# Splitting the seams between phases into two halves of the tokens, in an fp32 transformer kernel on one core

## Chip, core and metric

The kernel runs on one core of one Trainium2 chip. The metric is the device time in microseconds, the median of a few executions. The core has TensorE (PE in the profile, its weight loads PEld), VectorE (DVE), ScalarE (ACT), GpSimd (POOL) and SyncE (SP), which here issues only the weight loads from memory.

## What is computed

512 tokens of 1024 features go through two blocks in series, all in float32. The first has an even mixer, an odd mixer and two feed-forward parts with a causal convolution. The second has, twice over, a feed-forward part (FFN), a sparse-attention mixer and another FFN. Only the second block has a normalisation behind each part as well as before it, and that is what the change is about.  One part of the second block is

```python
def rms_norm_2(x, g):
    xf = x.astype(jnp.float32)
    y = xf * lax.rsqrt(jnp.mean(xf * xf, axis=-1, keepdims=True) + EPS)
    return (y * g.astype(jnp.float32)).astype(x.dtype)

def swiglu(x, w_gate, w_up, w_down):
    return (jax.nn.silu(x @ w_gate) * (x @ w_up)) @ w_down

# one part, six times (FFN, mixer, FFN, twice)
x = x + rms_norm_2(part(rms_norm_2(x, g_pre)), g_post)
```

(for an FFN the second summand is halved). The mean runs over the 1024 features of each token, so nothing of the next part can be multiplied before the last feature of this part's result is there: the place between two parts is called a seam below.

## The kernel before

Features lie on partitions (8 tiles of 128, a K tile), tokens on the free axis (512). `x`, `h_hi`, `h_lo` and `y` are [128, 8, 512]. Every product is made three times for accuracy: an operand is split into a rounded high part and the rest, and `w_lo*h_hi`, `w_hi*h_lo`, `w_hi*h_hi` are added in PSUM. The weights come as chunks of 8 K tiles by 256 output features, 1 MB each, in a ring of four slots. SP loads a chunk when the product four chunks before is done (`chunk_done`), ACT makes `w_hi` (`split_next`, L632), POOL makes `w_lo` (L2403, four instructions a chunk). A chunk is 48 products of 512 columns (`chunk_products`, L425): 8 K tiles, two output tiles of 128 features, three each. A group is the 256 output features that share an accumulator (`main`, two PSUM banks); a `Count` object keeps the semaphore values of each engine.

The order on each engine is the order in which the code is written; every engine runs its own list and they meet at semaphores. The last part of each list around a seam:

- The result of a part is four groups (m = 0 to 3). An FFN's group has three chunks (8, 8 and 6 K tiles, `DOWN_K`), a mixer's has one. `result_scalar` squares each group's banks (L712, L715, L719, L722), `result_vector` copies them with the gain to `y` (L854, `gained`) and adds the squares up in `acc`.
- The last chunk of the last group is `chunk_halves` (L551, products L562): all K tiles of the first output tile, then all of the second. Two K tiles before the end, `first_sums` (L574) sums over the features: `token_sums` (L485) are four matmuls with one column, tokens in the stationary operand. Behind the last product come `last_sums` (L580: the second bank's squares, four more such matmuls) and `spread` (L497).
- `norm_std` on ACT makes the root (L640), `norm_diag` (L744) on DVE the reciprocal (`col`, tokens on partitions, four columns) and then four diagonal matrices `diag = ident * col` (L749). `spread` multiplies them by ones (L501), which lays one factor per token over all partitions, in the bank `m[1]`. `keep_busy` (L568, L571) puts 5 and 9 matmuls without use before and behind it.
- For each K tile DVE scales `y` (L902), adds it to `x` (L904) and makes `h_lo` (L898), while ACT makes `h_hi` (L731) and, between them, the squares of the new `x` for the next norm (L734, L736, L740). DVE adds these up (L778) and joins the two banks (`join_banks`, L770).
- `first_pair` (L510) is the next part's first two chunks side by side, K tile by K tile (L521, L522, L526): 12 products of 512 columns a tile as `h_hi` and `h_lo` come. Before the eighth tile stands `sum_squares`, which waits for the joined squares. The third chunk's K tile 1 carries the `spread` of that next norm.
- Behind the sixth part (`norm` is None) there is no next part: DVE scales and adds four pairs of tiles (L887, L891) and `last_scalar` (L2488) stores each pair.

Every other norm of the kernel (the norms before parts, the head norms of the odd mixer, two half norms in the attention mixer) uses diagonals too.

## Time and profile before

| | |
|---|---|
| median of 3 runs | 3286.05 us (3285.17 to 3287.16) |
| the profiled execution | 3287.62 us, of which the span of the core is 3285.8 us |
| PE busy | 3212.9 us, 98% of the span |
| DVE, ACT, POOL busy | 37%, 36%, 44% |
| PE products of 512 columns on line 425 | 72% of the chain of work that ended last |
| granted TensorE clock, mean | 0.991 |

PE is the engine that sets the time, so a seam is read by what PE starts when: the distance between the starts of two neighbouring products is the slot that each takes, and whatever stands between two products beyond a slot is the seam's cost. A bar's own length (0.39 us) is longer than its slot, because matmuls are pipelined. A timeline line gives start, length, engine, source line, operation, what is written and read, and in brackets the idle time before it with its releaser.

### The profile page before, as it was taken

How to read it: one execution, taken by the hardware profiler on the slowest of the kernel's cores; microseconds unless marked ns; L12 is line 12 of the kernel's file. 1: busy time of each engine (PE TensorE's matmuls, PEld its weight loads, DVE VectorE, ACT ScalarE, POOL GpSimd, SP SyncE). 2: the span in 40 equal slices, each digit the busy share in tenths (PEclk: the TensorE clock that was granted, in tenths of full speed). 3: DMA queues.
4: the chain of work that ended last, by engine and by line, in shares of the span. 5: the costliest groups of instructions: out<-in, count | busy, mean ns of one | idle time of the engine just before them, and what ended most of it. 6: DMA issues, size and time to landing. Idle time of an engine off the chain costs nothing.

```text
span 3285.8 us, 39684 instructions
## 1 busy us (share of the span) xinstructions
PE 3212.9 (98%) x15940; PEld 2643.4 (80%) x15940; DVE 1205.1 (37%) x1807; ACT 1181.5 (36%) x1404; POOL 1456.3 (44%) x1112
## 2 busy tenths in 40 slices
PE   8999999999999999999899999999999989999998
PEld 6878888888888888888776888888888877788887
DVE  6534331343433112211847522114221374752212
ACT  4544432433443233222427433224222242743322
POOL 4335444432555444444550354454444372054443
PEclk9999999999999999999999999999999999999999
DMA  4213222211222222223320132222222241022222
GB/s 147 78 52 107 97 100 105 100 59 65 95 97 100 105 97 95 102 91 114 130 81 22 52 116 89 102 103 90 98 94 103 85 154 69 5 99 90 102 97 96
DMA packets 46235, 302.57 MB, mean 92 GB/s; under 512 B 5392, under 2 KB 7440, under 8 KB 10784
## 3 DMA queue, kind: packets, MB, share of 16 engines
q1 hardware_dynamic: 41040, 292.79, 24.9%
q10 hardware_dynamic: 5072, 7.96, 0.8%
q8 instruction: 99, 1.62, 0.2%
q14 instruction: 24, 0.20, 0.0%
HBM read 296.54 MB, written 2.10 MB: 91 GB/s over the span
## 4 chain that ended last, share of the span: by engine, by line
PE 89%; DVE 7%; ACT 2%; DMA 1%; issue 1%; ACTq 0%; DVEq 0%; SPq 0%
PE main L425 72%; PE main L442 3%; PE main L562 2%; PE main L1923 1%; PE misc L485 1%; PE main L521 1%; PE main L522 1%; PE main L526 1%; PE misc L521 1%; PE misc L522 1%; PE misc L526 1%; DVE b_p L2298 1%; ACT b_p L2079 1%; DVE b_flat L2164 1%; DMA stage<-in_w 0%
## 5 line engine op out<-in xcount | busy, mean ns | idle before, releaser
L2403 POOL TENSOR_TENSOR w_lo<-stage,w_hi 128x512 fp32r<-128x512 f32 x1104 | 1451.0, 1347 | 1793.5 <-ACT w_hi L632 1793.0
L425 PE MATMUL main<-h_hi,w_lo 128*128 128x512 f32 x2456 | 966.2, 393 | 8.6 <-DVE val L2111 6.3
L425 PE MATMUL main<-h_hi,w_hi 128*128 128x512 f32 x2456 | 960.5, 391 | 0.0
L425 PE MATMUL main<-h_lo,w_hi 128*128 128x512 f32 x2456 | 960.5, 391 | 0.0
L632 ACT ACTIVATE w_hi<-stage 128x2048 fp32r<-128x2048 f32 x276 | 524.7, 1909 | 408.6 <-DMA stage<-in_w 407.7
L425 PEld LDWEIGHTS main<-h_hi,w_lo 128*128 128x128 f32 x2456 | 464.2, 189 | 108.8 <-DVE val L2111 6.8
L425 PEld LDWEIGHTS main<-h_hi,w_hi 128*128 128x128 f32 x2456 | 463.8, 189 | 97.1
L425 PEld LDWEIGHTS main<-h_lo,w_hi 128*128 128x128 f32 x2456 | 464.3, 189 | 96.0 <-issue 0.5
L425 PE MATMUL main<-hid_hi,w_lo 128*128 128x512 f32 x1168 | 454.5, 389 | 0.0
L425 PE MATMUL main<-hid_hi,w_hi 128*128 128x512 f32 x1168 | 454.4, 389 | 0.0
L425 PE MATMUL main<-hid_lo,w_hi 128*128 128x512 f32 x1168 | 454.4, 389 | 0.0
L425 PEld LDWEIGHTS main<-hid_hi,w_lo 128*128 128x128 f32 x1168 | 219.3, 188 | 45.9 <-issue 0.2
L425 PEld LDWEIGHTS main<-hid_lo,w_hi 128*128 128x128 f32 x1168 | 219.3, 188 | 45.4
L425 PEld LDWEIGHTS main<-hid_hi,w_hi 128*128 128x128 f32 x1168 | 219.3, 188 | 45.3
L821 DVE TENSOR_TENSOR val<-main,rstd 128x1024 f32<-128x1024 f32 x60 | 73.5, 1224 | 461.4 <-PE main L425 461.4
L685 ACT ACTIVATE hid_hi<-val 128x1024 f32 (+1 forms) x66 | 69.9, 1059 | 372.2 <-DVE val L827 372.2
L801 DVE TENSOR_TENSOR gate<-main,rstd 128x1024 f32<-128x1024 f32 x66 | 80.8, 1225 | 318.5 <-PE main L425 301.7
L854 DVE TENSOR_SCALAR y<-main,par 128x512 f32<-128x512 f32 x48 | 36.0, 750 | 378.2 <-PE main L425 330.2
L831 DVE TENSOR_TENSOR hid_lo<-val,hid_hi 128x1024 f32 (+1 forms) x66 | 89.4, 1355 | 91.2 <-ACT hid_hi L685 91.2
L680 ACT ACTIVATE sq<-gate 128x1024 f32<-128x1024 f32 x44 | 46.7, 1061 | 185.5 <-DVE gate L819 185.0
L846 DVE TENSOR_TENSOR x<-main,x 128x1024 f32<-128x1024 f32 x16 | 19.6, 1225 | 245.8 <-PE main L425 245.8
L814 DVE SCALAR_TENSOR_TENSOR sq<-gate,par,sq 128x512 f32<-128x512 f32 x88 | 72.6, 846 | 45.2 <-ACT sq L673 39.1
(342 smaller groups left out, 3242.2 us busy)
## 6 DMA issues: line engine op xcount, KB each, us to landing
stage<-in_w SPq DMA_DIRECT2D x276, 1024.0 KB, 4.8
x<-in_xT SPq DMA_DIRECT2D x4, 512.0 KB, 8.1
out_x<-x ACTq DMA_DIRECT2D x4, 512.0 KB, 2.7
stage<-in_w SPq DMA_DIRECT2D x4, 256.0 KB, 8.2
b_r<-sq ACTq DMA_DIRECT2D x4, 256.0 KB, 6.9
b_r<-sq ACTq DMA_DIRECT2D x4, 255.5 KB, 8.4
ev_ws<-in_ev_ws ACTq DMA_DIRECT2D x1, 512.0 KB, 7.0
b_pos<-in_pos ACTq DMA_DIRECT2D x2, 256.0 KB, 2.7
```

Of the source, the lines that this page charges most:

```text
L425: last = pe.matmul(acc[:, m, :], w[a], r[b], start=start and k == 0 and j == 0, stop=stop and k == nk - 1 and j == 2)
L442: last = pe.matmul(out, x[:, k, r], w[:, s, k, :], start=k == 0 and t % 2 == 0 and j == 0, stop=k == KT - 1 and t % 2 == 1 and j == 2)
L521: pe.matmul(accs[j][:, m, :], w[1], c.h_hi[:, k, :], start=k == 0, stop=False)
L522: pe.matmul(accs[j][:, m, :], w[0], c.h_hi[:, k, :], start=False, stop=False)
L526: last = pe.matmul(accs[j][:, m, :], c.w_hi[:, slots[j], k, m * P:(m + 1) * P], c.h_lo[:, k, :], start=False, stop=k == KT - 1)
L632: act.activation(c.w_hi[:, s, :, :].rearrange("p k n -> p (k n)"), c.stage[:, s, :], ACT.Copy)\
L685: e.activation(two(c.hid_hi, i), c.val[:, :, :], ACT.Copy).then_inc(c.hid_hi_done, 1)
L801: e.tensor_tensor(c.gate[:, :, 2:], c.ps[n.slot()][:, :, :], rstd, ALU.mult)\
L814: e.scalar_tensor_tensor(c.sq[:, j, :], c.gate[:, j, k:k + T], c.par[:, bass.ds(col + 2 * i + j, 1)], c.sq[:, j, :], ALU.mult, ALU.add).th ...
L821: e.tensor_tensor(c.val[:, :, :], (c.mp[1] if extra else c.ps[n.slot()])[:, :, :], rstd, ALU.mult)\
L831: e.tensor_tensor(two(c.hid_lo, i), c.val[:, :, :], two(c.hid_hi, i).bitcast(F32), ALU.subtract).then_inc(c.hid_lo_done, 1)
L2403: last = e.tensor_tensor(c.w_lo[:, s, k:k + 2, :].rearrange("p k n -> p (k n)"), c.stage[:, s, k * CW:(k + 2) * CW], c.w_hi[:, s, k:k + 2, ...
```

## The change

Three things are changed together.

1. **The last result group is done in token halves.** The 512 tokens are cut into two `HALF`s of 256. All products of the last group's chunks are made at 256 columns (`half_products`), each half accumulating in its own PSUM bank: first half 0 of all chunks, then half 1. Half 0's squares, sums (`half_sums`, six matmuls now in place of four, since DVE no longer adds the last squares to `acc`), root, reciprocal and `half_spread` are hung between the products of half 1 (`half_hooks`, at the fifth and twelfth K step).
2. **The next pair takes four K tiles in halves.** `first_pair` walks K tiles 0 to 3 for half 0, then the same for half 1 (again 256 columns), then tiles 4 to 7 at 512. The sums and the spread of half 1 stand before its second and third step. DVE and ACT follow the same walk: scale, add, `h_hi`, `h_lo` of four half tiles, then those of half 1, then full tiles. `keep_busy` is gone from the seam. At the very end of the kernel the elementwise work and the stores are cut in halves too.
3. **Factors are spread without diagonals,** in every norm of the kernel: the stationary operand is one column of the factor repeated 128 times, the moving one is the identity (`spread_columns`). The four diagonal instructions on DVE (on ACT in the odd mixer) are gone.

```diff
+def spread_columns(pe, c, bank, cols):
+    for i in range(TT):
+        last = pe.matmul(bank[:, i * P:(i + 1) * P], cols[:, i:i + 1].to_broadcast([P, P]), c.ident[:, :],
+                         start=True, stop=True)
+    return last
 def spread(pe, n, c):
-    for i in range(TT):
-        pe.wait_ge(c.diag_ready, n(c.diag_ready))
-        last = pe.matmul(c.m[1][:, i * P:(i + 1) * P], c.ones[:, :], c.diag[:, i, :], start=True, stop=True)
-    last.then_inc(c.spread_ready, 1)
+    pe.wait_ge(c.rstd_ready, n(c.rstd_ready))
+    spread_columns(pe, c, c.m[1], c.col[:, 0:4]).then_inc(c.spread_ready, 1)
...
-    for k in range(KT):
-        if k == KT - 1:
+    walk = [(k, slice(0, T)) for k in range(KT)]
+    if n.halves:
+        walk = [(k, cols) for cols in HALF for k in range(EARLY)] + walk[EARLY:]
+    for p, (k, cols) in enumerate(walk):
+        if n.halves and p == 1:
+            half_sums(pe, n, c, 1)
+        if n.halves and p == 2:
...
+        if final:
             sum_squares(pe, n, c)
...
-                pe.matmul(accs[j][:, m, :], w[1], c.h_hi[:, k, :], start=k == 0, stop=False)
-                pe.matmul(accs[j][:, m, :], w[0], c.h_hi[:, k, :], start=False, stop=False)
+                pe.matmul(accs[j][:, m, cols], w[1], c.h_hi[:, k, cols], start=p == 0, stop=False)
+                pe.matmul(accs[j][:, m, cols], w[0], c.h_hi[:, k, cols], start=False, stop=False)
...
+HALF = (slice(0, CW), slice(CW, T))
+EARLY = 4
+def half_products(pe, c, acc, hi, lo, s, nk, k0, half, start, stop, at={}):
     for m in range(2):
         for k in range(nk):
-            if m == 1 and k == nk - 2:
...
+            if m * nk + k in at:
+                at[m * nk + k]()
+            out = acc[:, half, m * CW:(m + 1) * CW]
             w = (c.w_hi[:, s, k, m * P:(m + 1) * P], c.w_lo[:, s, k, m * P:(m + 1) * P])
-            r = (hi[:, k0 + k, :], lo[:, k0 + k, :])
+            r = (hi[:, k0 + k, HALF[half]], lo[:, k0 + k, HALF[half]])
...
-                last = pe.matmul(acc[:, m, :], w[a], r[b], start=start and k == 0 and j == 0,
-                                 stop=k == nk - 1 and j == 2)
-        last.then_inc((c.bank0_done, c.chunk_done)[m], 1)
...
+    return last
+def half_columns(c, half):
+    return c.m[0][:, 0:2] if half == 0 else c.m[1][:, T - 2:T]
+def half_sums(pe, n, c, half):
+    pe.wait_ge((c.p_sqa, c.p_sqb)[half], n((c.p_sqa, c.p_sqb)[half], 4))
+    src = [c.acc[:, 0, HALF[half]], c.sq[:, half, HALF[0]], c.sq[:, half, HALF[1]]]
+    for q, x in enumerate(src):
+        for u in range(2):
+            last = pe.matmul(half_columns(c, half)[:, u:u + 1], x[:, u * P:(u + 1) * P], c.ones[:, 0:1],
+                             start=q == 0 and u == 0, stop=q == 2 and u == 1)
+    last.then_inc(c.ssq_ready, 1)
+def half_bank(c, half):
+    return c.m[0][:, HALF[1]] if half == 0 else c.m[1][:, HALF[0]]
+def half_spread(pe, n, c, half):
+    pe.wait_ge(c.rstd_ready, n(c.rstd_ready))
+    for u in range(2):
+        last = pe.matmul(half_bank(c, half)[:, u * P:(u + 1) * P],
+                         c.col[:, 2 * half + u:2 * half + u + 1].to_broadcast([P, P]), c.ident[:, :],
+                         start=True, stop=True)
+    last.then_inc(c.spread_ready, 1)
...
-def last_sums(pe, n, c):
-    pe.wait_ge(c.p_sqb, n(c.p_sqb, 4))
-    token_sums(pe, c.m[0], c.ones, c.sq[:, 1, :], False, True).then_inc(c.ssq_ready, 1)
-    keep_busy(pe, c, 5)
-    spread(pe, n, c)
-    keep_busy(pe, c, 9)
+def half_hooks(pe, n, c, sums, spread):
+    def first():
+        pe.wait_ge(c.p_total, n(c.p_total))
+        half_sums(pe, n, c, 0)
+    return {sums: first, spread: lambda: half_spread(pe, n, c, 0)}
...
-            if post is not None and g == 3 and j == 2:
-                chunk_halves(pe, n, c, acc, c.hid_hi, c.hid_lo, nk, 8 * j, False, lambda: first_sums(pe, n, c))
-            else:
-                chunk_products(pe, n, c, acc, c.hid_hi, c.hid_lo, nk, 8 * j, j == 0, j == 2)
-    if post is not None:
-        last_sums(pe, n, c)
+            chunk_products(pe, n, c, acc, c.hid_hi, c.hid_lo, nk, 8 * j, j == 0, j == 2)
+    n.halves = post is not None
+    if post is None:
+        return
+    slots = [(n.chunk + j) % RING for j in range(3)]
+    def part(j, half, at={}):
+        return half_products(pe, c, acc, c.hid_hi, c.hid_lo, slots[j], DOWN_K[j], 8 * j, half, j == 0, j == 2, at)
+    pe.wait_ge(c.w_lo_done, n(c.w_lo_done))
+    part(0, 0)
+    part(0, 1).then_inc(c.chunk_done, 1)
+    pe.wait_ge(c.w_lo_done, n(c.w_lo_done))
+    part(1, 0)
+    pe.wait_ge(c.w_lo_done, n(c.w_lo_done))
+    part(2, 0).then_inc(c.bank0_done, 1)
+    part(1, 1, half_hooks(pe, n, c, 4, 11)).then_inc(c.chunk_done, 1)
...
         else:
+            act.wait_ge(c.p_add, n(c.p_add))
+            act.activation(c.col[:, 4:5], c.eps, ACT.Sqrt)
             act.wait_ge(c.bank0_done, n(c.bank0_done))
-            act.wait_ge(c.p_add, n(c.p_add))
             act.activation(c.sq[:, 0, :], acc[:, 0, :], ACT.Square).then_inc(c.p_sqa, 1)
-            act.activation(c.col[:, 4:5], c.eps, ACT.Sqrt)
-            act.wait_ge(c.chunk_done, n.chunk - AHEAD)
-            act.activation(c.sq[:, 1, :], acc[:, 1, :], ACT.Square).then_inc(c.p_sqb, 1)
+    def std(half):
+        u = slice(2 * half, 2 * half + 2)
+        act.wait_ge(c.ssq_ready, n(c.ssq_ready))
+        act.activation(c.col[:, u], half_columns(c, half), ACT.Sqrt, bias=c.eps, scale=1.0 / D).then_inc(c.std_ready, 1)
...
+    def second_squares():
+        act.wait_ge(c.chunk_done, n.chunk - AHEAD)
+        act.activation(c.sq[:, 1, :], acc[:, 1, :], ACT.Square).then_inc(c.p_sqb, 1)
     n.skip(c.group_taken, 4)
-    norm_std(act, n, c)
-    n.skip(c.spread_ready)
+    n.skip(c.spread_ready, 2)
+    std(0)
     if norm is None:
+        second_squares()
+        std(1)
         return
-    for k in range(KT):
+    def high(k, cols):
         act.wait_ge(c.x_ready, n(c.x_ready))
         col = PC["norm"] + norm * 8 + k
...
+    for k in range(EARLY):
+        high(k, HALF[0])
+    second_squares()
+    std(1)
+    for k in range(KT):
+        high(k, HALF[1] if k < EARLY else slice(0, T))
+        next_squares(act, n, c, k)
     n.skip(c.acc_ready, 2)
...
+            dve.tensor_tensor(c.acc[:, 0, :], c.acc[:, 0, :], c.acc[:, 1, :], ALU.add).then_inc(c.p_total, 1)
             n.skip(c.chunk_done)
...
+    def gained_half(half):
+        col = PC["post"] + post * 8 + 6
+        dve.wait_ge((c.p_sqa, c.p_sqb)[half], n((c.p_sqa, c.p_sqb)[half]))
+        for b in range(2):
+            last = dve.tensor_scalar(c.y[:, 6 + b, HALF[half]], acc[:, half, b * CW:(b + 1) * CW],
+                                     c.par[:, col + b:col + b + 1], None, ALU.mult)
+        last.then_inc(c.post_y if half == 0 else c.group_taken, 1)
+    def half_rstd(half):
+        u = slice(2 * half, 2 * half + 2)
+        dve.wait_ge(c.std_ready, n(c.std_ready))
+        dve.reciprocal(c.col[:, u], c.col[:, u]).then_inc(c.rstd_ready, 1)
+    gained_half(0)
+    dve.wait_ge(c.post_y, n(c.post_y))
+    half_rstd(0)
...
+        for half in range(2):
+            if half == 1:
+                gained_half(1)
+                dve.wait_ge(c.group_taken, n(c.group_taken, 0))
+                half_rstd(1)
+            dve.wait_ge(c.spread_ready, n(c.spread_ready))
+            for m in range(4):
+                y, x = (two(t, m)[:, :, HALF[half]] for t in (c.y, c.x))
+                dve.tensor_tensor(y, y, over_tiles(half_bank(c, half)), ALU.mult).then_inc(c.post_y, 1)
...
+    def gain(k, cols, factor):
+        dve.tensor_tensor(c.y[:, k, cols], c.y[:, k, cols], factor, ALU.mult).then_inc(c.post_y, 1)
+        dve.wait_ge(c.post_y, n(c.post_y))
+        dve.tensor_tensor(c.x[:, k, cols], c.x[:, k, cols], c.y[:, k, cols], ALU.add).then_inc(c.x_ready, 1)
+        n.skip(c.x_ready)
+    dve.wait_ge(c.spread_ready, n(c.spread_ready))
+    for k in range(EARLY):
+        gain(k, HALF[0], half_bank(c, 0))
+        if k >= 1:
+            low(k - 1, HALF[0])
+    low(EARLY - 1, HALF[0])
+    gained_half(1)
+    half_rstd(1)
+    dve.wait_ge(c.group_taken, n(c.group_taken, 0))
+    dve.wait_ge(c.spread_ready, n(c.spread_ready))
+    both = c.mp[0][:, :, :].rearrange("p b t -> p (b t)")[:, CW:CW + T]
     for k in range(KT):
-        dve.tensor_tensor(c.y[:, k, :], c.y[:, k, :], c.m[1][:, :], ALU.mult).then_inc(c.post_y, 1)
-        dve.wait_ge(c.post_y, n(c.post_y))
-        dve.tensor_tensor(c.x[:, k, :], c.x[:, k, :], c.y[:, k, :], ALU.add).then_inc(c.x_ready, 1)
-        n.skip(c.x_ready)
+        if k < EARLY:
+            gain(k, HALF[1], half_bank(c, 1))
+        else:
+            gain(k, slice(0, T), both)
         if k == 7:
             dve.wait_ge(c.x_ready, n(c.x_ready, 0))
         if k >= 1:
-            low(k - 1)
+            low(k - 1, HALF[1] if k <= EARLY else slice(0, T))
         if k in (5, 7):
             gather_squares(dve, n, c, k // 2 - 1)
-    low(7)
...
     chunk_products(pe, n, c, group_slot(pe, n, c), c.hid_hi, c.hid_lo, KT)
-    chunk_halves(pe, n, c, group_slot(pe, n, c), c.hid_hi, c.hid_lo, KT, 0, True, lambda: first_sums(pe, n, c))
-    last_sums(pe, n, c)
+    acc = group_slot(pe, n, c)
+    pe.wait_ge(c.w_lo_done, n(c.w_lo_done))
+    s = n.chunk % RING
+    half_products(pe, c, acc, c.hid_hi, c.hid_lo, s, KT, 0, 0, True, True).then_inc(c.bank0_done, 1)
+    half_products(pe, c, acc, c.hid_hi, c.hid_lo, s, KT, 0, 1, True, True, half_hooks(pe, n, c, 4, 11))\
+        .then_inc(c.chunk_done, 1)
+    n.chunk += 1
...
-    act.wait_ge(c.stored, 64)
+    for half in range(2):
+        for m in range(4):
+            act.wait_ge(c.last_ready, 4 * half + m + 1)
+            act.dma_start(out[:, 2 * m:2 * m + 2, HALF[half]], c.x[:, 2 * m:2 * m + 2, HALF[half]])\
+                .then_inc(c.stored, 16)
+    act.wait_ge(c.stored, 128)
```

The other diagonals (odd mixer on ACT, attention mixer on DVE) are removed in the same way; the weight ring and the loops inside the parts are as they were.

On PE, around the first seam (FFN to mixer), the end of the last group before, where L485 are sums, L571 fillers, L501 the spread and L521 the pair:

```order
L485 MATMUL misc<-ones,acc 128x1 x4
L562 MATMUL main<-hid_hi,w_lo 128x512
L562 MATMUL main<-hid_lo,w_hi 128x512
L562 MATMUL main<-hid_hi,w_hi 128x512
L562 MATMUL main<-hid_hi,w_lo 128x512
L562 MATMUL main<-hid_lo,w_hi 128x512
L562 MATMUL main<-hid_hi,w_hi 128x512
L485 MATMUL misc<-ones,sq 128x1 x4
L571 MATMUL misc<-ones,ident 128x128 x5
L501 MATMUL misc<-diag,ones 128x128 x4
L571 MATMUL misc<-ones,ident 128x128 x9
L521 MATMUL main<-h_hi,w_lo 128x512
```

and the same place after, at the mixer-to-FFN seam where the rows are shortest: L561 the last product of half 1, L535, L536 and L540 the pair's first and second half tile, L577 the six sums of half 1, L591 its spread comes one half tile later:

```order
L561 MATMUL main<-hid_hi,w_hi 128x256
L535 MATMUL main<-h_hi,w_lo 128x256
L536 MATMUL main<-h_hi,w_hi 128x256
L535 MATMUL main<-h_hi,w_lo 128x256
L536 MATMUL main<-h_hi,w_hi 128x256
L535 MATMUL misc<-h_hi,w_lo 128x256
L536 MATMUL misc<-h_hi,w_hi 128x256
L535 MATMUL misc<-h_hi,w_lo 128x256
L536 MATMUL misc<-h_hi,w_hi 128x256
L540 MATMUL main<-h_lo,w_hi 128x256 x2
L540 MATMUL misc<-h_lo,w_hi 128x256 x2
L577 MATMUL misc<-ones,acc 128x1 x2
```

Nothing stands between the last result product and the pair's first any more; the sums moved behind the pair's first half tile.

On DVE the same seam before, from the gain of the last bank (L854) over the reciprocal (L746) and the diagonals (L749) to the second K tile:

```order
L854 TENSOR_SCALAR y<-main,par 128x512 x2
L746 RECIPROCAL col<-col 128x4
L749 TENSOR_SCALAR diag<-ident,col 128x128 x4
L902 TENSOR_TENSOR y<-y,misc 128x512
L904 TENSOR_TENSOR x<-x,y 128x512
L902 TENSOR_TENSOR y<-y,misc 128x512
L904 TENSOR_TENSOR x<-x,y 128x512
L898 SCALAR_TENSOR_TENSOR h_lo<-x,par,h_hi 128x512
```

and after, from half 0's last `h_lo` (L965) through the gain of half 1 (L936) and its reciprocal (L943) to its first tiles (L969, L971):

```order
L971 TENSOR_TENSOR x<-x,y 128x256
L965 SCALAR_TENSOR_TENSOR h_lo<-x,par,h_hi 128x256 x2
L936 TENSOR_SCALAR y<-main,par 128x256 x2
L943 RECIPROCAL col<-col 128x2
L969 TENSOR_TENSOR y<-y,misc 128x256
L971 TENSOR_TENSOR x<-x,y 128x256
```

Half 0's chain stands ahead of all of half 1's on DVE. ACT has the same order: here the first four `h_hi` halves (L781) stand ahead of the squares of half 1 (L769), between the two roots (L765):

```order
L760 ACTIVATE sq<-main 128x512
L765 ACTIVATE col<-misc,stat 128x2
L781 ACTIVATE h_hi<-x,par 128x256 x4
L769 ACTIVATE sq<-main 128x512
L765 ACTIVATE col<-misc,stat 128x2
```

Before, the squares of the last bank had nothing but the other bank's squares and a constant's root ahead of them.

## Rows read from the trace of the kernel before

**Rows 1.** The page: span, and busy time of PE.

```profile
span 3285.8 us, 39684 instructions
PE 3212.9 (98%) x15940; PEld 2643.4 (80%) x15940; DVE 1205.1 (37%) x1807; ACT 1181.5 (36%) x1404; POOL 1456.3 (44%) x1112
```

**Rows 2.** Timeline of the first seam, FFN to mixer, PE, ACT and DVE.

```profile
1553.69 0.39 PE L562 MATMUL main<-hid_hi,w_hi 128*128 128x512 f32 x1
...
1554.72 0.49 PE L562 MATMUL main<-hid_hi,w_lo 128*128 128x512 f32 x1
...
1555.97 0.40 PE L562 MATMUL main<-hid_hi,w_hi 128*128 128x512 f32 x1
1556.41 0.60 ACT L722 ACTIVATE sq<-main 128x512 f32<-128x512 f32 x1 [2.90 <-PE main L562]
...
1560.27 0.69 DVE L902 TENSOR_TENSOR y<-y,misc 128x512 f32<-128x512 f32 x1 [0.66 <-PE misc L501]
...
1562.58 0.47 PE L521 MATMUL main<-h_hi,w_lo 128*128 128x512 f32 x1 [0.34 <-ACT h_hi L731]
```

**Rows 3.** The same timeline at the end of the pair.

```profile
1575.37 0.69 DVE L904 TENSOR_TENSOR x<-x,y 128x512 f32<-128x512 f32 x1
...
1579.66 5.47 POOL L2403 TENSOR_TENSOR w_lo<-stage,w_hi 128x512 fp32r<-128x512 f32 x4 [31.41 <-ACT w_hi L632]
...
1579.82 1.68 DVE L770 TENSOR_TENSOR acc<-acc 128x512 f32<-128x512 f32 x1
...
1585.40 0.40 PE L425 MATMUL main<-h_hi,w_lo 128*128 128x512 f32 x1
```

**Rows 4.** The chain that ended last: start, length, products without a gap.

```profile
71.65 11.50 PE main L442 x96
...
1219.50 327.78 PE main L425 x1446
```

**Rows 5.** Groups by line and shape: operations of 256 columns.

```profile
L2298 DVE CUSTOM_DVE_ANT_0 b_p<-main,b_amask 128x256 f32<-128x256 f32 x32 | 11.6, 421 | 0.0
L1565 DVE SCALAR_TENSOR_TENSOR od_s<-od_s,od_decays,misc 128x256 f32<-128x256 f32 x24 | 11.5, 481 | 5.6 <-PE misc L1332 3.8 <-DVE acc L1598 0.8 <-DVE val L1598 0.2
L2079 ACT ACTIVATE b_p<-b_p,b_nmax 128x256 f32<-128x256 f32 x32 | 15.8, 503 | 0.0
```

**Rows 6.** Timeline of the first mixer-to-FFN seam, PE.

```profile
1859.41 0.40 PE L562 MATMUL main<-hid_hi,w_hi 128*128 128x512 f32 x1
...
1866.01 0.47 PE L521 MATMUL main<-h_hi,w_lo 128*128 128x512 f32 x1 [0.34 <-ACT h_hi L731]
```

**Rows 7.** Timeline of the kernel's end: last product, first and last elementwise work.

```profile
3269.11 0.40 PE L562 MATMUL main<-hid_hi,w_hi 128*128 128x512 f32 x1
...
3273.39 2.35 DVE L887 TENSOR_TENSOR y<-y,misc 128x1024 f32<-128x1024 f32 x2 [0.66 <-PE misc L501]
...
3280.20 2.36 DVE L891 TENSOR_TENSOR x<-x,y 128x1024 f32<-128x1024 f32 x2
```

**Rows 8.** Timelines where diagonals are made: odd mixer, attention mixer, an FFN's third chunk.

```profile
687.81 1.16 PE L1379 MATMUL misc<-diag,ones 128*128 128x128 f32 x8 [2.19 <-ACT diag L1443]
...
1762.50 1.16 PE L1860 MATMUL misc<-diag,ones 128*128 128x128 f32 x8 [0.71 <-DVE diag L2316]
...
1890.19 0.83 PE L501 MATMUL misc<-diag,ones 128*128 128x128 f32 x6
...
1891.44 0.47 PE L425 MATMUL main<-h_hi,w_lo 128*128 128x512 f32 x1
```

**Rows 9.** Busy time in stretches of the odd mixer: PE, PEld, DVE, ACT, POOL, granted clock.

```profile
684.00:688.00 4.00, 1.81 (x9) 1.19 (x8) 1.74 (x3) 3.48 (x7) 3.27 (x3) 1.00 0.00 0
...
720.00:724.00 4.00, 4.00 (x13) 3.09 (x12) 0.18 (x1) 2.93 (x7) 3.86 (x4) 0.57 0.01 4
```

**Rows 10.** The chain again, in the odd mixer, ahead of the second stretch.

```profile
711.84 1.50 PE main L442 x12
...
717.05 1.95 PE misc L485 x16
```

153 lines of the change are left out of this document (49 added, 104 removed).

## The prediction, as it was made before the changed kernel ran

> **What bounds the kernel now.** I read the page first: PE is busy 98% of the span [rows 1], so an edit pays only where it shortens the distance between two PE products. Then the chain that ended last, for the price of a product: 1446 products of 512 columns took 327.78 us without a gap, 0.2267 us each, and 96 products of 256 columns took 11.50 us, 0.1198 us each [rows 4]. So a full product cut in two costs 2 x 0.1198 - 0.2267 = 0.0129 us more. Then the timeline of a seam. From the start of the last result product to the pair's first pass 1562.58 - 1555.97 = 6.61 us, of which 0.23 is a slot: 6.38 us of standing or filling [rows 2]. The mixer's seam has 1866.01 - 1859.41 = 6.60 [rows 6]; all five inner seams are alike. The first sums, in the stream, take the way from 1553.69 to 1555.97 for six slots, 2.28 - 1.36 = 0.92 us [rows 2]. A seam costs 7.30 us, five of them 36.5 us, and the end of the kernel has its own tail. That is all the change can reach, apart from the diagonals.
>
> **What an FFN seam costs after.** Three FFN seams (22 K tiles in the last group).
> - Width: 22 x 6 = 132 result products and 4 x 12 = 48 of the pair are cut in two: 180 x 0.0129 = 2.32 us.
> - Sums and spreads now all stand in the stream. The four sums cost 0.92, so about 0.20 each and 0.1 for the start; six cost 1.31, twice: 2.62. Two spread matmuls at the same 0.20: 0.50, twice: 1.00. The new stationary operand (one column repeated) has no row; bounds are the same price as the diagonal and twice the 0.20, which adds 0.8 us to a seam. I take the same, since the rows with a full 128x128 stationary show no dependence on the moving width.
> - The wait at the pair's first product. Let the last product of half 0 end its slot at 0. Squares (0.2 later, 0.60 long) are done at 0.9, before the sums' place at 12 x 0.12 = 1.44; sums end at 2.75, root and reciprocal at 3.5, and the spread stands at 1.44 + 1.31 + 21 x 0.12 = 5.27, so the factor is readable at about 5.9. Scale and add at 256 columns take 0.42 each (the PSUM reader of that width 421 ns, a three-operand one 481, ACT 503 [rows 5], against 0.69 at 512 [rows 2]): `x` at 6.8, `h_hi` at 7.4. The pair starts at (48 + 36) x 0.12 + 1.31 + 0.50 = 11.9. Nothing waits, with 4.4 us to spare. This is the cover that hides the whole first half; without it the 6.38 us come back.
> - The wait behind it. DVE needs, before, from its first scaling at 1560.27 to the end of the last `x` at 1576.06 15.8 us, and 5.44 more until the squares are joined at 1579.82 + 1.68 = 1581.50 [rows 2, 3]. PE reached its sums just then, without a wait. After, twelve of DVE's instructions (four tiles, three each) are half as wide and 0.265 shorter: 15.8 - 3.2 + 5.44 = 18.05 us from the spread of half 1. But PE has less to do in that time: 24 half products (2.88), 48 more (5.75) and 36 full ones (8.16), 16.8, less 0.18 until the factor can be read, 16.6. So PE stands 1.4 us before the eighth tile: half of the pair's DVE work used to run ahead of the pair, now only a part of it does. The third chunk's `w_lo`, ready 0.27 before its use [rows 3], moves with the same `x` and comes out level with PE again: no second wait.
> Sum: 2.32 + 2.62 + 1.00 + 1.4 = 7.34 against 7.30: nothing. The bound from below on the last wait is 0, if DVE's half instructions are shorter than the nearest rows, from above 2.4.
>
> **A mixer seam** (two of them) has 8 K tiles: 48 + 48 products cut, 1.24 us; sums and spreads 3.62; the wait at the eighth tile 1.4. The pair starts already at 48 x 0.12 + 1.81 = 7.6, just when the first half `h_hi` is there (7.4). But then come, on ACT and in this order, four half `h_hi` and only then half 1's squares. DVE needs 5.9 + 4.2 us for four tiles with their `h_lo`, so the fourth `h_hi` is done at 10.6 and the squares at 11.2. PE wants them at 7.6 + 1.44 = 9.1: it stands 2.1 us with the rest of the pair queued behind it. Sum 8.36 against 7.30: +1.06 each. Inner seams together: 3 x 0.04 + 2 x 1.06 = **+2.2 us**.
>
> **The end.** Width 132 x 0.0129 = 1.70; the sums and spread of half 0 in the stream 1.81 in place of 0.92: +0.9. From the last product at 3269.11 to the first scaling at 3273.39 pass 4.28 us [rows 7]; the sums get 0.4 longer, the spread 0.4 shorter, the first diagonal goes: -0.3. The elementwise work behind it, 3273.39 to 3282.56, 9.2 us for eight instructions of 1024 columns [rows 7], becomes eight of 512 in dependent pairs, 8 x 0.69 = 5.5: -3.7. The last store is half as large: 0 to -0.7, say -0.4. Together **-1.8 us**.
>
> **Diagonals.** Where PE waited for them they go: odd mixer 2.19 us of waiting [rows 8], of which the four ACT instructions are 1.3; attention mixer 0.71 us of wait and as long a DVE share behind it, 0.8 each, two times. In the third chunk of an FFN POOL runs beside and the four diagonals are late: the spread holds the stream 1.25 us, from 1890.19 to 1891.44, instead of 0.81 [rows 8]; that is 0.44 in three such places and about 0.5 in the odd mixer's. The others are made long before their use and are worth nothing. -1.3 - 1.6 - 1.8 = **-4.7 us**, between -2 and -6.
>
> **Sum:** 2.2 - 1.8 - 4.7 = -4.3 us. The profiled execution took 3287.62 us with 3285.8 of span; a like one would take 3283.3. The median of the runs is 1.57 below it, so the forecast for the median is 3286.05 - 4.3 = 3281.8 us.
>
> One rule is to be weighed. The rows give a slot of 0.2267 us at 512 columns and 0.1198 at 256 [rows 4], that is 13 ns above the columns at 2.4 GHz whatever the width. The Trainium skill, page "TensorE: Matmul & The Clock Gate", section "Back-to-back issue gap", gives 2.5 ns for that; by it a cut product costs 2.5 ns more and not 12.9, and the 864 cut products 2 us and not 11: 3272.8 us. The trace disagrees with the page, and the sum goes by the trace.
>
> **Rivals.**
> - *The cover holds and no wait takes its place.* If DVE's half instructions and ACT's order leave no wait at the eighth tile (5 x 1.4) and at the mixer's sums (2 x 2.1), 11.2 us more go: 3270.6. For it: I built both waits on prices taken from other lines. Against: they rest on rows of just this width [rows 5], and 1.4 us is a quarter of what DVE would have to gain. A part of it would already be measurable: 2.3 us below my forecast. In the same direction goes a smaller price of width, as above. Chance 0.29.
> - *The clock falls at the seams.* The fillers that kept PE at work are gone, and the standing at the eighth tile and at the mixer's sums comes right beside one-column sums. The granted clock fell to 0.57 over 4 us after PE had stood from 713.34 to 717.05, 3.7 us [rows 9, 10], which costs 1.7 us of products; around the wait of 2.2 us it was 1.00 [rows 8, 9]. With 1.7 us behind each of the seven standings: 3281.8 + 12 = 3294: slower. It decides from standings of between 2.2 and 3.7 us; mine are 1.4 and 2.1. Chance 0.08. The Trainium skill says the same direction, in the same page's section "Why this matters for your kernels": avoid idle gaps of TensorE between bursts of matmuls, or it goes back to the half clock.
> - *A half product waits for its stationary operand.* The weight load is 0.19 us long in the trace, longer than the 0.12 slot. If it did not overlap here, all 1728 half products would cost 0.07 more, +121 us: 3403. The 96 products of 256 columns at 0.1198 [rows 4] load a stationary as large and speak plainly against. With a slower column load of the spreads in it: chance 0.04.
> - *The pair is not released early*, since half 0's factor comes too late: the mixer seam has 0.2 us to spare there. 1 us late would add 2 us: 3284, inside my range.
>
> **How the numbers follow.** Forecast 3281.8, chance 0.59 with what the unknown prices leave around it (3279.5 to 3290). A difference under 0.2%, 6.6 us, is about what a measurement of this kernel can't tell from no change: faster is below 3279.5, slower above 3292.6. Faster 0.29 (the first rival, whole or half), same 0.59, slower 0.12 (clock, stationary operand). The range 3272 to 3290 leaves out the whole of the first rival below and the two slower ones above.
>
> **What would show it.** In the profile after: products of L561 and the pair's 256-column ones 0.12 us apart; the pair's first product one slot behind the last of L561; a wait of about 1.4 us at the sums before the eighth tile, five times, on DVE's L826; a wait of about 2.1 us at L577 in the two mixer seams, on ACT's L769; the spreads with the column at 0.10 us a record; the granted clock 1.00 across each seam; the distance from the last product to the span's end shorter by some 4 us. The prediction is wrong if one of the two waits is missing, if the clock falls, or if other work behind the seam moves, such as a weight chunk that comes late in the third chunk.

## The result, and the profile after

The changed kernel is slower: 3289.71 us (median of 20 runs, 3285.72 to 3295.71) beside 3283.82 us for the kernel before (20 runs), ratio 1.0017, 95% interval 1.0011 to 1.0023: +5.9 us where -4.3 was forecast. That is within the 0.2% called "same", but on the other side of zero. One execution of one kernel below (`cover_tile8`) took 9404 us at a granted clock of 0.332; the ratios leave it out.

The page of the changed kernel, as [rows 1] was of the one before:

```profile
span 3293.0 us, 41186 instructions
...
PE 3220.2 (98%) x16684; PEld 2684.1 (82%) x16684; DVE 1179.1 (36%) x1807; ACT 1183.9 (36%) x1414; POOL 1457.7 (44%) x1112
```

The span of the profiled execution is 7.2 us longer than that of before. Most of what the forecast built is there. PE's timeline of the first seam, where [rows 2] showed 6.61 us between the last product and the pair's first (start, length, engine, line, operation):

```profile
1558.55 0.28 PE L561 MATMUL main<-hid_hi,w_hi 128*128 128x256 f32 x1
1558.67 0.28 PE L535 MATMUL main<-h_hi,w_lo 128*128 128x256 f32 x1
...
1560.11 0.50 PE L577 MATMUL misc<-ones,acc 128*128 128x1 f32 x4
1560.47 1.03 PE L577 MATMUL misc<-ones,sq 128*128 128x1 f32 x8
...
1562.88 0.60 PE L591 MATMUL misc<-ident,col 128*128 128x128 f32 x4
```

The pair starts one slot of 0.12 us behind the last result product. The two waits that the forecast put in its place are there too, at their sizes. PE's waits (who waits for whom: total, times, longest):

```profile
PE misc L485 <- DVE acc L826: 6.7, 6, 1.4
...
PE misc L577 <- ACT sq L769: 4.5, 3, 1.9
```

1.35 us before the eighth K tile (forecast 1.4), 1.9 at half 1's sums in the two mixer seams (forecast 2.1; the third is the end's 0.69). Where the new time lies is read from one event that both kernels have, the sums before the eighth tile, at the five seams; first before, then after:

```profile
1581.74 0.95 PE L485 MATMUL misc<-ones,acc 128*128 128x1 f32 x8
...
1885.18 0.95 PE L485 MATMUL misc<-ones,acc 128*128 128x1 f32 x8
...
2253.94 0.95 PE L485 MATMUL misc<-ones,acc 128*128 128x1 f32 x8
...
2622.70 0.95 PE L485 MATMUL misc<-ones,acc 128*128 128x1 f32 x8
...
2926.11 0.95 PE L485 MATMUL misc<-ones,acc 128*128 128x1 f32 x8
```

```profile
1581.66 1.05 PE L485 MATMUL misc<-ones,acc 128*128 128x1 f32 x8 [1.35 <-DVE acc L826]
...
1891.19 1.05 PE L485 MATMUL misc<-ones,acc 128*128 128x1 f32 x8 [0.91 <-DVE acc L826]
...
2259.73 0.49 PE L485 MATMUL misc<-ones,acc 128*128 128x1 f32 x3 [1.36 <-DVE acc L826]
...
2628.24 1.05 PE L485 MATMUL misc<-ones,acc 128*128 128x1 f32 x8 [1.35 <-DVE acc L826]
...
2933.54 1.05 PE L485 MATMUL misc<-ones,acc 128*128 128x1 f32 x8 [1.35 <-DVE acc L826]
```

The differences are -0.1, +6.0, +5.8, +5.5 and +7.4 us: the two FFN seams in the middle add nothing (-0.2 and -0.3, of which -0.4 each is the third chunk without its diagonals); the loss lies between the first pair's eighth tile and the first mixer seam's, and again from the second mixer on. The stretches there, with the granted clock (PE, PEld, DVE, ACT and POOL busy, then the granted clock, third from the right, and the DMA):

```profile
1580.00:1584.00 4.00, 2.65 (x16) 2.11 (x15) 1.79 (x3) 0.26 (x1) 4.00 (x4) 0.98 0.10 7
1584.00:1588.00 4.00, 4.00 (x13) 3.14 (x12) 0.00 (x0) 0.00 (x0) 1.21 (x1) 0.60 0.36 99
1864.00:1868.00 4.00, 2.11 (x16) 1.90 (x14) 3.47 (x9) 1.50 (x3) 0.00 (x0) 0.89 0.72 262
1868.00:1872.00 4.00, 4.00 (x20) 4.00 (x21) 0.17 (x1) 0.26 (x1) 0.00 (x0) 0.50 0.00 0
1872.00:1876.00 4.00, 4.00 (x28) 4.00 (x28) 2.79 (x8) 1.70 (x3) 0.00 (x0) 0.76 0.00 0
...
2932.00:2936.00 4.00, 2.65 (x15) 2.17 (x15) 1.67 (x2) 1.65 (x2) 4.00 (x4) 0.94 0.00 0
2936.00:2940.00 4.00, 4.00 (x13) 3.15 (x12) 0.00 (x0) 0.00 (x0) 4.00 (x4) 0.64 0.16 20
```

Three times the clock goes down to its lower level of 1.2 GHz right behind one of the new standings (behind the eighth tile's at 1581.66 and 2933.54, behind the 1.9 us at 1866.86), and (1 - clock) x 4 us summed over each group gives 1.7, 3.4 and 1.7 us, 6.8 in all. (Inside the first mixer, ahead of 1753 us, the distance to before grew by another 1.4 us. Before has two falls of the clock there and this trace has four, besides the one at 1584 us; that they are the 1.4 us is argued, not shown.) From the sums at 2926.11 and 2933.54 to the end of the span are 359.7 us before and 359.5 after; the later one contains the third of these falls (+1.7) and a third chunk without diagonals (-0.4), so the end itself gave -1.5. From the last result product to the span's end pass 12.5 us where it was 16.7, the 4 us less that the forecast named.

### The profile page after: what moved, and what is told of

It reads as the page before. It is cut to its first block, busy times and chain, and to the rows that moved or that the text cites. A ratio compares the mean times of both kernels' runs of the same rounds, so it can differ in the third digit from the quotient of the medians.

```text
span 3293.0 us, 41186 instructions
## 1 busy us (share of the span) xinstructions
PE 3220.2 (98%) x16684; PEld 2684.1 (82%) x16684; DVE 1179.1 (36%) x1807; ACT 1183.9 (36%) x1414; POOL 1457.7 (44%) x1112
## 4 chain that ended last, share of the span: by engine, by line
PE 88%; DVE 9%; ACT 2%; issue 1%; DMA 0%; SPq 0%; DVEq 0%; ACTq 0%
PE main L425 70%; PE main L561 4%; PE main L442 3%; PE main L1992 1%; DVE acc L834 1%; ACT b_p L2152 1%; DVE x L971 1%; DVE y L969 1%; DVE b_p L2371 1%; PE misc L485 1%; DVE h_lo L965 1%; PE main L535 1%; PE misc L500 1%; PE misc L577 1%; PE misc L1872 0%
## 5 line engine op out<-in xcount | busy, mean ns | idle before, releaser
L425 PE MATMUL main<-hid_hi,w_lo 128*128 128x512 f32 x1040 | 404.7, 389 | 0.0
L425 PE MATMUL main<-hid_hi,w_hi 128*128 128x512 f32 x1040 | 404.6, 389 | 0.0
L425 PE MATMUL main<-hid_lo,w_hi 128*128 128x512 f32 x1040 | 404.6, 389 | 0.0
L425 PEld LDWEIGHTS main<-hid_hi,w_lo 128*128 128x128 f32 x1040 | 195.2, 188 | 40.7 <-issue 0.2
L425 PEld LDWEIGHTS main<-hid_lo,w_hi 128*128 128x128 f32 x1040 | 195.2, 188 | 40.6
L425 PEld LDWEIGHTS main<-hid_hi,w_hi 128*128 128x128 f32 x1040 | 195.2, 188 | 40.5
L910 DVE TENSOR_SCALAR y<-main,par 128x512 f32<-128x512 f32 x36 | 27.0, 751 | 354.0 <-PE main L425 330.3
L561 PE MATMUL main<-hid_hi,w_lo 128*128 128x256 f32 x416 | 118.7, 285 | 0.0
L561 PE MATMUL main<-hid_hi,w_hi 128*128 128x256 f32 x416 | 117.7, 283 | 0.0
L561 PE MATMUL main<-hid_lo,w_hi 128*128 128x256 f32 x416 | 117.7, 283 | 0.0
```

Source lines behind the costliest of these rows:

```text
L425: last = pe.matmul(acc[:, m, :], w[a], r[b], start=start and k == 0 and j == 0, stop=stop and k == nk - 1 and j == 2)
L561: last = pe.matmul(out, w[a], r[b], start=start and m == 0 and k == 0 and j == 0, stop=stop and m == 1 and k == nk - 1 and j == 2)
```

## Experiments

A standing is a stretch in which PE waits with nothing to do; a fall is a stretch at the lower clock; a cover is work without use that fills a standing. Two theories at the start. **A:** PE's standings of 1 to 2 us bring the clock down, and the fillers (`keep_busy`) and the old order kept it up at the seams. **B:** the falls of the clock come and go by themselves, and a kernel of other timing meets others. "Against the changed kernel" is a difference of two ratios to before, times 3284 us; an interval of such a difference is about 4 us wide on either side of nothing, so only the larger ones say much by themselves.

**The spreads alone**, the third part of the change in the kernel before.

> The kernel before with nothing changed but the factors: no diagonals, each spread is a product of the broadcast column and the identity. The forecast took this part for -4.7 us (odd mixer -1.3, attention mixers 2 x -0.8, three third chunks and one place of the odd mixer -1.8). Theory A (the clock takes back what the odd mixer gains: PE still stands 1 us before the head's sums, the clock falls behind it and comes back at the same moment of the program as in the kernel before): the odd mixer gives nothing at its end, the attention mixers 2 x -0.8, the third chunks -0.4 each: -2.5 us, between -1.5 and -3.3, and a granted clock of under 0.65 in 716 to 724 us. Theory B (the clock plays no part in it; what went missing in the changed kernel went missing in the seams): -4.7 us, between -4 and -5.5, and the 1.7 us gained by 717 us are still there at 725 us.

```diff
+    pe.wait_ge(c.rstd_ready, n(c.rstd_ready))
+    spread_columns(pe, c, c.m[1], c.col[:, 0:4]).then_inc(c.spread_ready, 1)
...
```

Measured: 3278.58 us, ratio 0.9983 (0.9974 to 0.9992), -5.6 us. The median lies at the forecast's -4.7 and theory B's range; the interval, -8.5 to -2.6, also reaches into theory A's (-1.5 to -3.3), so the time alone does not decide. The traces speak against "given back": the same product runs 4.5 us earlier than in before both ahead of head 1's sums (684.73 and 689.27 us) and behind the fall (719.23 and 723.74), and each trace has one fall there. But they also say how such a thing arises. Clock in the odd mixer of before, beside [rows 9], and then of the spreads alone:

```profile
752.00:756.00 4.00, 3.02 (x19) 2.66 (x18) 0.20 (x1) 3.75 (x3) 0.83 (x1) 0.81 0.47 199
756.00:760.00 4.00, 4.00 (x10) 3.13 (x11) 0.18 (x1) 3.22 (x7) 4.00 (x4) 0.50 0.00 0
760.00:764.00 4.00, 4.00 (x21) 3.16 (x21) 1.22 (x1) 0.00 (x0) 0.13 (x1) 0.84 0.00 0
```

```profile
752.00:756.00 4.00, 4.00 (x17) 3.28 (x16) 0.18 (x1) 1.43 (x2) 3.63 (x3) 0.61 0.00 0
```

The same standing (head 2's, 0.98 us) is followed by (0.19 + 0.50 + 0.16) x 4 = 3.4 us of lost clock in one execution and by (0.04 + 0.39) x 4 = 1.7 in the other, whose clock is 0.96 in the 4 us ahead of this row and 1.00 in the next rows.

**Before without its fillers.**

> The kernel before without its 5 + 9 filling products at each post-norm seam; nothing else changed. They write a bank that nobody reads. Theory A (standings beside one-column sums bring the clock down, and the fillers kept it up): behind most of the five inner seams the products run at half rate for 3 us or so, 1.7 us each at least; +5 to +12 us, granted clock of about 0.6 in the 4 us behind a seam. Theory B (the clock's falls in the changed kernel come from when its standings happen, not from missing fillers): within 1 us of before, the clock 1.00 behind the seams as it is now.

```diff
...
-    keep_busy(pe, c, 5)
     spread(pe, n, c)
-    keep_busy(pe, c, 9)
```

Measured: 3298.85 us, ratio 1.0042 (1.0028 to 1.0056), +13.8 us, a little above the upper end of theory A. Where the fillers stood PE now stands, and the clock falls behind it:

```profile
PE main L521 <- ACT h_hi L729: 11.8, 5, 2.4
...
PE misc L501 <- DVE diag L747: 6.4, 9, 1.0
```

```profile
1552.00:1556.00 4.00, 1.65 (x9) 1.39 (x9) 3.27 (x6) 1.14 (x2) 0.00 (x0) 0.78 0.35 145
1556.00:1560.00 4.00, 4.00 (x11) 3.03 (x11) 3.93 (x7) 2.42 (x4) 0.00 (x0) 0.50 0.02 4
```

It fell so at all five inner seams. In the seams as they were, with PE waiting up to 2.4 us for the pair's first operand, the fillers that the change removed were worth 14 us, and no line of the forecast's sum had them. What they would be worth in the new seams, where the pair waits for nothing, this run does not show. The same pair of traces speaks for a part of B: up to 1553 us the two programs are alike instruction by instruction, yet the sums that stand at 1213.41 us in before stand at 1205.96 here:

```profile
1205.96 0.95 PE L485 MATMUL misc<-ones,acc 128*128 128x1 f32 x8
```

7.45 us between two executions of the same code, 6.7 of them in three places where the clock fell in the one (at 24 to 36, 720 to 724 and 752 to 764 us) and not at all in the other.

**The changed kernel with its standings covered.**

> The changed kernel with cover where PE stands in its inner seams: six products of 512 columns (1.36 us, into the result slot that is already free) ahead of the sums before the eighth K tile in all five seams, and in the two mixer seams sixteen repeats of the pair's first 256-column product (1.92 us) before the pair. Nothing else is changed; the waits of 1.4 and 1.9 us shrink to 0 to 0.4. Theory A: the granted clock stays at 1.00 through the seams that lost 1.7, 4.0 and 2.9 us, and 5 to 8 us of the time come back: 3282 to 3285 us for a kernel that takes 3289.7, about 1.000 of before. Theory B: the clock falls all the same, or the fillers only push the pair back: no gain, 3289 to 3292 us, 1.0015 to 1.0025 of before.

```diff
         if final:
+            if n.halves:
+                pe.wait_ge(c.group_taken, n(c.group_taken, 0))
+                for _ in range(6):
+                    pe.matmul(c.ps[n.slot()][:, 0, :], c.w_hi[:, slots[0], 0, 0:P], c.h_hi[:, 0, :],
+                              start=True, stop=True)
             sum_squares(pe, n, c)
         pe.wait_ge(c.h_hi_done, n(c.h_hi_done))
+        if p == 0:
+            for _ in range(n.fill):
+                pe.matmul(accs[0][:, 0, cols], c.w_lo[:, slots[0], k, 0:P], c.h_hi[:, k, cols], start=True, stop=True)
```

(`n.fill` is 16 in the mixer seams and 0 in the others.) Measured: 3280.24 us, ratio 0.9989 (0.9980 to 0.9998): -9.2 us against the changed kernel, from products that compute nothing. The stretch that had 0.98 and 0.60, and the mixer seam:

```profile
1576.00:1580.00 4.00, 4.00 (x21) 3.30 (x21) 0.18 (x1) 0.27 (x1) 3.13 (x3) 1.00 0.25 82
...
1856.00:1860.00 4.00, 4.00 (x34) 3.83 (x33) 1.97 (x6) 1.26 (x3) 0.00 (x0) 1.00 0.54 229
```

No seam of this trace has a clock under 1.00. Theory A holds for the seams.

**Only the eighth tile covered** (the first hunk alone), to tell the standings of 1.35 us from those of 1.9.

> The changed kernel with only the first half of the cover: six products of 512 columns (1.36 us) ahead of the sums before the eighth K tile in the five inner seams; the mixer seams' wait of 1.9 us at half 1's sums stays uncovered. In the trace of the changed kernel the clock fell behind the eighth tile's standing in the first FFN seam (1580 to 1588) and in the second mixer seam (2932 to 2940), and behind the standing of 1.9 us in the first mixer seam (1864 to 1876). Theory A1 (a standing of 1.4 us is enough when one-column sums follow it): the falls behind the eighth tile are gone, that behind the 1.9 us stays: 4 to 6 of the 9 us that the full cover gave, 3283.5 to 3286 us. Theory A2 (only the standings of 1.9 us matter): 0 to 2 us, 3287.5 to 3290 us.

Measured: 3283.72 us, ratio 1.0001 (0.9991 to 1.0010), -5.3 us against the changed kernel; the other cover is the remaining -3.9. That is theory A1's forecast (3283.5 to 3286): standings of 1.35 us are enough. In its trace both uncovered mixer seams lose clock, the first as in the changed kernel:

```profile
1852.00:1856.00 4.00, 2.13 (x16) 1.93 (x15) 3.75 (x10) 1.82 (x4) 0.00 (x0) 0.92 0.66 240
1856.00:1860.00 4.00, 4.00 (x20) 4.00 (x21) 0.25 (x2) 0.26 (x1) 0.00 (x0) 0.50 0.06 23
```

**Half 1's squares earlier in the mixer seams.**

> The changed kernel with ACT's order changed in the two mixer seams alone: half 1's squares between the second and the third half h_hi, not behind the fourth. The forecast's account of the 1.9 us wait (ACT's order sets it) says: the sums are ready when PE comes to them. DVE still makes half 1's reciprocal only after its four tiles, done some 6.3 us after the first gain; PE, 1.9 us earlier at the spread, stands there for 0.6 to 0.8 us. So 1.9 turns into 0.7: -1.2 us each, -2.4 in all, and with the shorter standing the clock may stay up behind one or both seams, up to 3 us more: 3284.5 to 3287.5 us. Against it, if DVE sets the wait and not ACT's order: the whole 1.9 us comes back at the spread, 3289 to 3290.5 us.

```diff
     for k in range(EARLY):
+        if k == EARLY - 2 and chunks == 1:
+            second_squares()
         high(k, HALF[0])
-    second_squares()
+    if chunks > 1:
+        second_squares()
```

Measured: 3284.01 us, ratio 0.9993 (0.9984 to 1.0002), -7.9 us against the changed kernel, at the good end and beyond. ACT's order did set the wait, and it is gone whole; of the 0.6 to 0.8 us that I expected at the spread only 0.2 came:

```profile
1861.52 1.03 PE L577 MATMUL misc<-ones,sq 128*128 128x1 f32 x8
...
1864.10 0.71 PE L591 MATMUL misc<-ident,col 128*128 128x128 f32 x4
```

Neither line has a wait at its end, and the spread starts 0.18 us later behind the products ahead of it than in the first FFN seam. 2 x 1.9 us are saved, and with them the fall behind. Not every fall goes with them: behind the eighth tile's standing of the second seam, 1.36 us here, the clock now falls (at 1884 us), where it had stood only 0.91 us and kept its clock in the changed kernel.

**Products between the one-column sums**, the standing left as it is.

> The changed kernel with the 1.4 us before the eighth tile's sums left standing, but with one product of 512 columns behind each of the four one-column sums (4 x 0.23 us more work in each of five seams, up to +4.5 us). It asks whether the standing or the one-column sums behind it bring the clock down. If the standing alone does: the falls stay, 1.0017 of before plus 0.0013: 3293 to 3294.5 us. If it takes the sums' 0.9 us of nearly idle engine as well: the falls behind the eighth tile go as in cover_tile8 (-5.2 us) and 4.5 are paid: 3288.5 to 3290 us, and the clock is 1.00 at 1580 to 1592 us and behind the second mixer seam's eighth tile.

```diff
+def spaced_sums(pe, n, c, slot):
...
+    for i in range(TT):
+        last = pe.matmul(c.m[0][:, i:i + 1], c.acc[:, 0, i * P:(i + 1) * P], c.ones[:, 0:1],
+                         start=i == 0, stop=i == TT - 1)
+        pe.matmul(c.ps[n.slot()][:, 0, :], c.w_hi[:, slot, 0, 0:P], c.h_hi[:, 0, :], start=True, stop=True)
...
-        if final:
+        if final and n.halves:
+            spaced_sums(pe, n, c, slots[0])
+        elif final:
             sum_squares(pe, n, c)
```

Measured: 3292.66 us, ratio 1.0024 (1.0014 to 1.0035), the median nearer to "the standing alone" (3293) than to the other (3290), the interval too wide to decide. The trace decides the place:

```profile
1577.56 0.38 PE L496 MATMUL misc<-ones,acc 128*128 128x1 f32 x2 [1.35 <-DVE acc L840]
1577.80 0.48 PE L498 MATMUL main<-h_hi,w_hi 128*128 128x512 f32 x1
...
1579.78 0.63 PE L550 MATMUL main<-h_hi,w_hi 128*128 128x512 f32 x1
1580.21 0.63 PE L549 MATMUL main<-h_hi,w_lo 128*128 128x512 f32 x1
```

With wide products among the sums the clock still fell: from 1579.8 a product takes 0.43 us and not 0.23. At this place the standing does it without the sums' nearly idle engine. At the second mixer seam the fall behind the eighth tile was absent, but PE had stood less there than in the changed kernel (1.35 us), because a fall of the clock ahead had made it late:

```profile
2931.81 0.38 PE L496 MATMUL misc<-ones,acc 128*128 128x1 f32 x2 [1.06 <-DVE acc L840]
```

So for the other seams the question stays open.

**Head 0's sums one K tile later in the odd mixer.**

> The changed kernel with head 0's sums in the odd mixer one K tile later (6 products of 0.23 us moved ahead of them) and its spread one tile later too. Nothing else is changed. PE stood 1.0 us there, with the clock at 0.60 and 0.54 in 716 to 724 us behind it. Theory A: without the standing the clock stays at 1.00 there, the 1.7 us that the absent diagonals gave are kept, and the standing itself goes: -1.7 - 1.0 = -2.7 us against the changed kernel, between -2 and -4. Theory B (the clock falls behind the sixteen one-column sums themselves, with or without a standing): -1.0 us, between 0 and -1.2, and the clock under 0.65 as before.

```diff
-    z(at={2: lambda: sums(0), 5: lambda: spread_head(0)})
+    z(at={3: lambda: sums(0), 6: lambda: spread_head(0)})
```

Measured: 3286.36 us, ratio 1.0002 (0.9993 to 1.0011), -4.9 us (by the medians -3.3; theory A had -2 to -4). The size fits within the noise, the reason given does not: I had taken the sums at 717 us for head 0's, and they are head 1's. Head 0's stood 1.0 us at 679 us, with the clock at 1.00 behind. Head 1's standing is still there in this run's trace (0.98 us at 713.80), and the clock does not fall behind it.

**The best of the parts.** Three more kernels put together what paid: first the spreads and the end in halves, with the inner seams of before.

> The kernel before with the spreads by columns and with the last seam alone, the one behind which no pair follows, in token halves: 132 products of the last group cut in two, sums, factor, scaling and stores by half. The five inner seams are as before, with their fillers. The forecast's price of the end is -1.8 us (in the trace of the changed kernel -1.95): 3278.6 - 1.9 = 3276.7 us, 0.9975 to 0.998 of before. If the halves at the end only looked cheap because the changed kernel's clock was lower or higher there: no difference from the spreads alone, 3278 to 3279 us.

Measured: 3279.41 us, ratio 0.9980 (0.9971 to 0.9989). Against the spreads alone that is -1.0 us by the ratios and +0.8 by the medians: not told apart, and above the 3276.7 that was expected. In the traces the distance from the last seam's sums (2915.13 and 2921.89 us) to the span's end is 359.4 and 357.7 us, -1.7, as priced.

> As spreads_end, and in the odd mixer head 0's sums and spread one K tile later (as in odd_later). There that gave 3.3 us against the changed kernel by the medians, 1.0 us of it the standing. If the clock's fall behind that standing is what the rest was: again -2.7 to -3.3, 3273.5 to 3274.5 us, and the granted clock of 712 to 724 us is 1.00. If the gain in odd_later was the run's luck: -1.0, 3275.7 us. Both kernels would then be slower than this one by 0.3%.

Measured: 3275.05 us, ratio 0.9974 (0.9964 to 0.9985), between the two values that were expected, 3274.5 and 3275.7: undecided. Its PE row for head 1 and the clock behind it, and then the same with head 1's sums moved too:

```profile
714.02 1.95 PE L485 MATMUL misc<-ones,sq 128*128 128x1 f32 x16 [0.98 <-ACT sq L1548]
...
716.00:720.00 4.00, 4.00 (x19) 3.29 (x18) 0.18 (x1) 2.61 (x3) 4.00 (x4) 1.00 0.02 4
```

> spreads_end_odd with head 1's sums and spread one K tile later as well. A correction to what was expected of odd_later belongs here: head 0's sums are those at 679 us of the trace of before, and the ones at 717 us, behind which the clock was at 0.57, are head 1's. Moving head 0's took away a standing of 1.0 us at 679 us; that of head 1 was still there (0.98 us at 714.0) and the clock nevertheless stayed at 1.00 behind it in that trace, as it had not in seven of the nine others. So a standing of 1 us brings the clock down in some executions and not in others. If that is so, head 1's move gives its 1.0 us and the share of executions in which the clock fell there, some 0.7 x 1.5 to 2 us: -2 to -2.5 us, 3272.5 to 3273 us, and clock 1.00 in 708 to 724 us. If the clock falls behind the sixteen one-column sums alone: -1.0 us, 3274 us, and the clock under 0.7 at 712 to 720 us.

```diff
-    z(at={2: lambda: sums(1), 5: lambda: spread_head(1)})
+    z(at={3: lambda: sums(1), 6: lambda: spread_head(1)})
```

```profile
713.25 1.84 PE L485 MATMUL misc<-ones,sq 128*128 128x1 f32 x16
...
716.00:720.00 4.00, 4.00 (x24) 3.45 (x22) 0.18 (x1) 1.63 (x3) 3.88 (x4) 1.00 0.00 0
```

Measured: 3273.13 us, ratio 0.9967 (0.9957 to 0.9976): faster than before by 10.8 us, and than the changed kernel by 16. It is the fastest of the study. Against spreads_end_odd it is -2.3 us, as expected, but too little to be told from nothing by itself. The sixteen sums without a standing leave the clock at 1.00; with the standing it was 1.00 in the trace above too, so this pair does not separate the two.

> The changed kernel with three repairs together: six filling products of 512 columns before the eighth tile's sums (cover_tile8), half 1's squares earlier in the mixer seams (squares_early; there the wait of 1.9 us went to zero), and head 0's sums and spread in the odd mixer one K tile later (odd_later). Against the full cover (0.9989 of before), in which the 1.9 us were filled and not saved: -2 x 1.9 us for the squares, -1.5 to -3.3 us for head 0: 3274 to 3276 us, 0.9967 to 0.9975 of before. If the three gains were only luck of the clock, each taking back the other's: 3279 to 3281 us. Beside spreads_end_odd (the same kernel with the inner seams of before, 0.9974) it tells what the halves of the inner seams are worth once they are covered: by the sum 3 x +0.25 for the FFN seams and 2 x -0.75 for the mixer seams, -0.75 us, so nothing that can be told from zero.

Measured: 3275.90 us, ratio 0.9976 (0.9967 to 0.9985), at the upper end of what was expected (3276 us, 0.9975). With every repair the halves in the inner seams end where the old inner seams with their fillers are (0.9974): their worth is not told from nothing, +0.02% with an interval of 0.14% to either side.

**Theory A and B together.** In the odd mixer the standing is always 0.98 us. Over the twelve other traces (all but odd_later_two), head 1's, at some 713 to 717 us, was followed by a fall of the clock in 9; head 2's, near 750 us, in 8 of 13; head 0's, near 679 us, in 1 of the 9 traces that have it. Before the eighth tile there are 20 uncovered places (four kernels, five seams). In 16 of them PE stood 1.34 to 1.37 us, and a fall followed in 8: in all four first seams, in the four mixer seams among them, and in none of the eight middle FFN seams. In the other 4, mixer seams behind a fall at half 1's sums, it stood 0.45 to 1.06 us, and no fall followed. The uncovered 1.9 us were followed by one in 6 of 8. So a standing does bring the clock down (A), but not each, and not equally long (what B had right). Why the middle seams differ so steadily from the others was not settled.

## Why the prediction was wrong

By its steps, in order. **Slots and widths** held: 0.12 us a half product, the pair one slot behind. **Seams**, read from the covered kernel against the spreads alone, between the same sums on either side (both have the spreads): the three FFN seams +0.05, +0.27 and +0.21 us where +0.04 was forecast, the two mixer seams +1.13 and +1.16 where it was +1.06. **The waits**, 1.4 and 2.1: 1.35 and 1.9, on the lines named. **The end**, -1.8: -1.5 here, -1.7 in spreads_end. **Diagonals**, -4.7: -5.6, with an interval of 3 us to either side; in the traces the wait in the odd mixer gave 1.3, as forecast, and the third chunk's spread holds the stream 0.81 us, from 1896.36 to 1897.17, where it was 1.25 (forecast -0.44). The spread by a column costs as much as the one by a diagonal, as assumed; [rows 8] has its answer here:

```profile
686.09 1.16 PE L500 MATMUL misc<-ident,stat 128*128 128x128 f32 x8 [0.90 <-DVE stat L1656]
...
1896.36 1.05 PE L500 MATMUL misc<-ident,col 128*128 128x128 f32 x8
```

2.19 us of wait have become 0.90 (forecast -1.3).

Together these give what the forecast's sum says, and they are not what failed. Take the ratios: the change as a whole is +5.6 us, the spreads are -5.6 and the end some -1.5, so the inner seams cost +12.7, give or take 4, where the sum had +2.2. With cover they cost 9.2 less, +3.5. **The clock at the seams is the rest**: the second rival was the case. It had +12 us for seven falls of 1.7; 9.2 came back with the cover. The changed kernel's one trace has three falls there, 6.8 us, and grew by another 1.4 us in the first mixer, which no run isolates.

The step that failed is this one: "The granted clock fell to 0.57 over 4 us after PE had stood from 713.34 to 717.05, 3.7 us", and with it "It decides from standings of between 2.2 and 3.7 us; mine are 1.4 and 2.1", which pressed the rival's chance to 0.08. PE did not stand for 3.7 us there. The numbers come from the chain of work that ended last [rows 10]; it leaves PE at 713.34 because the sums were waiting for DVE and ACT, and says nothing of what PE did meanwhile. PE's own timeline of before does:

```profile
715.68 0.39 PE L425 MATMUL main<-h_hi,w_hi 128*128 128x512 f32 x1
717.05 1.95 PE L485 MATMUL misc<-ones,sq 128*128 128x1 f32 x16 [0.98 <-ACT sq L1433]
```

It worked until 716.07 and stood 0.98 us. A fall behind 0.98 us stood in the trace of before; read so, both new standings lie above the least that was seen to matter, and the rival had to be weighed like the forecast itself. The one clear place of 2.2 us without a fall [rows 8, 9] showed only that not every standing does it. A second omission goes with it: the 5 + 9 fillers were priced by the time that they free and not by what they keep up, which no_fillers puts at 13.8 us for the old seams.

The Trainium skill, page "TensorE: Matmul & The Clock Gate", section "HAM oscillation — how this bites in real kernels", tells of a kernel whose every K tile starts at the lower clock because PE waits between tiles. That is the direction seen here; its waits are longer than any of these seams', and here standings of 0.98 us (18 of 34 places), 1.35 us (8 of 16) and 1.9 us (6 of 8) were enough.

## What to carry over

Where an engine looks idle in the chain of waits, read its own timeline before a threshold is built on it: the chain shows who was waited for, not who stood still. Work without use ahead of a wait can be worth more than the wait: before it is taken out, price it by removing it alone. And a single profile of a kernel whose clock comes and goes is one draw: two executions of the same code differed by 7.45 us here, more than the whole effect, so small changes need medians, and traces are for places.
